# A 32-bit encoder block on one core: gate and up as seven half-token products of block sums, FFN in three groups

## What is computed

```
def rms_norm(x, g):
    xf = x.astype(jnp.float32)
    y = xf * lax.rsqrt(jnp.mean(xf * xf, axis=-1, keepdims=True) + NORM_EPS)
    return (y * g.astype(jnp.float32)).astype(x.dtype)

def swiglu(h, w_gate, w_up, w_down):
    return (jax.nn.silu(h @ w_gate) * (h @ w_up)) @ w_down
...
        x = x + 0.5 * swiglu(rms_norm(x, ffn1_norm[i]), ffn1_w_gate[i], ffn1_w_up[i], ffn1_w_down[i])
        h = rms_norm(x, mix_norm[i])
        proj = h @ w_in[i]
...
        x = x + jnp.concatenate([y_ssd, y_pool], axis=-1) @ w_out[i]
        x = x + 0.5 * swiglu(rms_norm(x, ffn2_norm[i]), ffn2_w_gate[i], ffn2_w_up[i], ffn2_w_down[i])
    return rms_norm(x, final_norm)
```

## Time and profile before

| | |
|---|---|
| median of 3 runs | 1042.38 us (1042.3 to 1042.4) |
| the profiled execution | 1042.32 us, of which the span from the first to the last instruction 1040.6 us |
| granted TensorE clock | 0.997 of full |
| busy: PE, DVE, ACT, POOL | 1031.2, 559.6, 380.4, 179.1 us |
| FFN1's first output tile is done, last unit of the mixer ends | VectorE reads their banks at 268.71 and 667.04 us |

### The profile page before, as it was taken

The page is one execution under the profiler, slowest core; times in us unless marked ns, Lnnn a source line. Parts: engine busy times, 40 slices in busy tenths (PEclk is TensorE's granted clock), DMA queues, the critical chain, the costliest instruction groups (busy, mean ns, idle before and its releaser), DMA issues.

```text
span 1040.6 us, 13577 instructions
## 1 busy us (share of the span) xinstructions
PE 1031.2 (99%) x4798; PEld 847.3 (81%) x4798; DVE 559.6 (54%) x686; ACT 380.4 (37%) x489; POOL 179.1 (17%) x166
## 2 busy tenths in 40 slices
PE   9999999999999999999999999999999999999997
PEld 7888888888888878878787888888888888888887
DVE  5544444444344468786799795554444444433432
ACT  6433223322333337652234753432333223332332
POOL 1110110101001032221063451110101101101100
PEclk9999999999999999999999999999999999999998
DMA  6533323322333343222222233333333332233222
GB/s 184 150 113 101 101 86 95 101 83 68 99 98 96 101 124 100 82 81 70 73 81 81 62 101 101 101 101 90 92 101 101 96 87 89 79 109 95 86 68 81
DMA packets 188873, 99.09 MB, mean 95 GB/s; under 512 B 3780, under 2 KB 188200, under 8 KB 188840
## 3 DMA queue, kind: packets, MB, share of 16 engines
q1 hardware_dynamic: 188168, 97.60, 32.3%
q10 hardware_dynamic: 672, 1.05, 0.3%
HBM read 96.54 MB, written 2.10 MB: 95 GB/s over the span
## 4 chain that ended last, share of the span: by engine, by line
PE 96%; DVE 3%; issue 1%; ACT 1%; POOL 0%; ACTq 0%; POOLq 0%
PE bank L1150 29%; PE bank L1152 29%; PE bank L1151 29%; PE bank L1222 1%; PE bank L1216 1%; PE bank L1219 1%; PE bank L1471 1%; PE bank L1284 0%; PE bank L1306 0%; PE bank L1472 0%; PE bank L1473 0%; PE bank L1274 0%; DVE w_lo_part L743 0%; DVE ebuf L903 0%; PE bank L1190 0%
## 5 line engine op out<-in xcount | busy, mean ns | idle before, releaser
L1150 PE MATMUL bank<-xghi,w_hi_part 128*128 128x512 f32 x960 | 377.4, 393 | 0.0
L1152 PE MATMUL bank<-xghi,w_lo_part 128*128 128x512 f32 x960 | 373.8, 389 | 0.0
L1151 PE MATMUL bank<-xglo,w_hi_part 128*128 128x512 f32 x960 | 373.6, 389 | 0.0
L743 DVE TENSOR_TENSOR w_lo_part<-w_raw,w_hi_part 128x1024 fp32r<-128x1024 f32 x194 | 253.9, 1309 | 192.8 <-ACT w_hi_part L498 187.5
L498 ACT ACTIVATE w_hi_part<-w_raw 128x1024 fp32r<-128x1024 f32 x194 | 203.8, 1051 | 196.2 <-PE bank L1152 194.7
L1150 PEld LDWEIGHTS bank<-xghi,w_hi_part 128*128 128x128 f32 x960 | 180.2, 188 | 39.9 <-issue 2.8
L1151 PEld LDWEIGHTS bank<-xglo,w_hi_part 128*128 128x128 f32 x960 | 180.3, 188 | 38.4 <-issue 1.2
L1152 PEld LDWEIGHTS bank<-xghi,w_lo_part 128*128 128x128 f32 x960 | 180.2, 188 | 37.5
L1150 PE MATMUL bank<-acthi,w_hi_part 128*128 128x512 f32 x330 | 130.5, 396 | 0.0
L410 POOL TENSOR_TENSOR gate_buf<-gate_buf,rstd 128x512 f32<-128x512 f32 x44 | 57.1, 1298 | 424.5 <-ACT gate_buf L521 424.5
L1152 PE MATMUL bank<-acthi,w_lo_part 128*128 128x512 f32 x330 | 129.4, 392 | 0.0
(11 more groups left out here) (223 smaller groups left out, 805.0 us busy)
## 6 DMA issues: line engine op xcount, KB each, us to landing
w_raw<-in_ffn_w_gate SPq DMA_DIRECT2D x42, 512.0 KB, 3.8
w_raw<-in_ffn_w_up SPq DMA_DIRECT2D x42, 512.0 KB, 3.8
w_raw<-in_w_in SPq DMA_DIRECT2D x29, 512.0 KB, 3.8
w_raw<-in_ffn_w_down SPq DMA_DIRECT2D x32, 384.0 KB, 3.2
w_raw<-in_ffn_w_down SPq DMA_DIRECT2D x32, 320.0 KB, 3.0
w_raw<-in_w_out SPq DMA_DIRECT2D x16, 512.0 KB, 3.6
out<-xtok SPq DMA_DIRECT2D x4, 512.0 KB, 3.4
xload<-in_x SPq DMA_DIRECT2D x3, 512.0 KB, 7.0
```

Of the source, the lines that this page charges most:

```text
L743: dve.tensor_tensor(wlo[:, slot(m)], raw[:, slot(m)], whi[:, slot(m)].bitcast(F32), ALU.subtract).then_inc(w_lo, 1)
L1150: pe.matmul(bank, w, h, start=first and n == 0, stop=False)
L1151: pe.matmul(bank, w, l, start=False, stop=False)
L1152: mm = pe.matmul(bank, wl, h, start=False, stop=last and n == blocks - 1)
```

## The change

**Gate and up.** For most hidden tiles two tiles are taken together (a quad: gate and up of two tiles, four raw weight slots). The 8 feature blocks are split into two halves of four, the two tiles are the other split, and the tokens are split into two halves of 256. The four weight quarters and the four activation quarters then make a 2 x 2 by 2 x 2 product, done with seven products instead of eight, on sums and differences of quarters. Each product is 24 matmuls of 256 columns: 8 for gate and up times four blocks, times 3 for the parts. Of the 22 tile pairs of both FFNs, 19 are quads; the first 4 tiles of FFN1 and the first 2 of FFN2 stay as they were ("direct").

**Sums of weights.** Four VectorE instructions of 128 x 1024 for a quad (`first_sum` to `fourth_sum`), and a high and a low part for each of the seven products. There are eight raw slots in place of four.

**Sums of activations.** Four combinations of 128 x 256 for each of four block pairs of `xT`, made once for an FFN: `halves_of_x` and `combination_hi` on ScalarE, `combine` and `combine_low` on VectorE. In FFN1 they stand in the four direct steps from the fifth item on; for FFN2 in the last four steps of the mixer.

**Results.** ScalarE copies three partial products out of PSUM, VectorE adds three later ones to them (`gather`), GpSimd scales three gates of 256 tokens by `rstd`.

**Groups.** Hidden tiles go in groups of 8, 8 and 6; behind each group all eight output tiles get that group's part. Each part is one unit of 8 or 6 blocks, scaled on VectorE by half of `rstd` into `upd` and added to `xT` in a second instruction. VectorE forms a weight's low part two items ahead of the running one, where it was three; ScalarE stays three ahead. In the last tile's halves only the third group's 6 blocks are left, where there were 22, and `finish` for the first half stands behind 3 blocks of the second half, where it stood behind 6. The loops of the FFNs are written out.

The core of the diff:

```diff
+        def weight(q, part):
+            quad = QUADS[q]
+            slot0 = quad.raw % RAW
+            if part in (SUM1, SUM4):
+                return wsum[:, 0]
+            if part == SUM2:
+                return wsum[:, 1]
+            f1, k1 = part in (SUM3, A22), part in (A12, A22)
+            pair = raw[:, slot0 + 2 * f1:slot0 + 2 * f1 + 2, :, :].rearrange("p e k f -> p e (k f)")
+            return pair[:, :, k1 * KH * P:(k1 + 1) * KH * P]
...
+                    sp.wait_ge(w_lo, FREE[key])
+                if key[0] == 1 and slot >= RING:
+                    sp.wait_ge(unit_done, M_FFN2)
...
+            def scale_gate(q, i, h, done, ready):
+                pool.wait_ge(done, q + 1)
+                gate = post[:, q % 2, i, 0:HALF]
...
+            def halves_of_x(f, j, gain):
+                act.wait_ge(x_ready, DK * 2 * f + j + 1)
+                act.activation(b12[:, j, :], xT[:, j * S + HALF:(j + 1) * S], ACT.Copy,
+                               scale=par[:, one(gain + j)]).then_inc(b12_ready, 1)
+            def combination_hi(f, j):
+                act.wait_ge(t_own, 4 * (KH * f + j + 1))
+                act.activation(thi[:, :, j, :], t32[:, j, :, :], ACT.Copy).then_inc(t_hi, 1)
...
+            def copy_product(q, part, i, bank, ready, reader):
+                act.wait_ge(unit_done, QUADS[q].base + part + 1)
+                if q >= 2:
+                    act.wait_ge(reader, q - 1)
+                act.wait_ge(t_lo, KH * (QUADS[q].ffn + 1))
+                act.activation(post[:, q % 2, i, :], PB[bank][:, :], ACT.Copy).then_inc(ready, 1)
...
+            def combine(f, j, gain):
+                c = 4 * (KH * f + j)
+                low, high = xT[:, cols(j)], xT[:, cols(j + KH)]
+                g0, g4, neg4 = par[:, one(gain + j)], par[:, one(gain + KH + j)], neg_gain[:, f, KH + j:KH + j + 1]
+                dve.wait_ge(b12_ready, KH * f + j + 1)
+                def term(i, x, scalar, other, op):
+                    dve.scalar_tensor_tensor(out=t32[:, j, i, :], in0=x, scalar=scalar, in1=other,
+                                             op0=ALU.mult, op1=op).then_inc(t_own, 1)
+                term(0, low[:, 0:HALF], g0, b12[:, j, :], ALU.subtract)
+                term(2, high[:, HALF:S], g4, b12[:, j, :], ALU.subtract)
+                dve.wait_ge(t_own, c + 1)
+                term(1, high[:, HALF:S], neg4, t32[:, j, 0, :], ALU.subtract)
+                dve.wait_ge(t_own, c + 3)
+                term(3, high[:, 0:HALF], neg4, t32[:, j, 1, :], ALU.subtract)
+            def combine_low(f, j):
+                dve.wait_ge(t_hi, KH * f + j + 1)
+                dve.tensor_tensor(tlo[:, :, j, :], t32[:, j, :, :], thi[:, :, j, :].bitcast(F32),
+                                  ALU.subtract).then_inc(t_lo, 1)
...
+            def first_sum(q):
+                for j in (2, 3):
+                    w_landed(dve, (QUADS[q].ffn, QUADS[q].raw + j))
+                if q:
+                    before = QUADS[q - 1].base + SUM4 + 1
+                    dve.wait_ge(w_lo, before)
+                dve.tensor_tensor(weight(q, SUM1), weight(q, SUM3), weight(q, A22), ALU.add).then_inc(sum_ready[1], 1)
...
+            def gather(q, part, i, bank, read, ready):
+                dve.wait_ge(unit_done, QUADS[q].base + part + 1)
+                dve.wait_ge(read, q + 1)
+                c = post[:, q % 2, i, :]
+                dve.tensor_tensor(c, c, PB[bank][:, :], ALU.add).then_inc(ready, 1)
...
+            def down_scaled(f, g, d, rows=slice(0, S), bank=None):
+                use = 3 * DK * f + DK * g + d
+                if use >= 2:
+                    added(use - 2)
+                dve.scalar_tensor_tensor(out=upd[:, d % 2, rows], in0=bank if bank is not None else PB[4 + d % 2][:, :],
+                                         scalar=0.5, in1=rstd[:, rows], op0=ALU.mult,
+                                         op1=ALU.mult).then_inc(d_read, 1)
...
+                        gate21(q)
+                    if product and it.part == SUM1:
+                        fourth_sum(q)
...
+                    if product and it.part == SUM3:
+                        gather(q, A12, 0, 3, p1_read, c11_done)
+                    if product and it.part == SUM4:
+                        gather(q, SUM3, 1, q % 2, p5_read, c22_done)
+                    if product and it.part == A22:
+                        gather(q, SUM4, 2, 2, u2_read, c12_done)
+                    if before is not None and before.kind == "direct":
+                        direct_post(f, before, n - 1)
+                    if before is not None and before.kind == "down":
+                        update(f, before.group, before.d, last)
+                    if starts_quad(n + 3):
+                        first_sum(ffn_item(n + 3).quad)
+                    if starts_quad(n + 2):
+                        second_sum(ffn_item(n + 2).quad)
+                    if converted <= n + 2 < M_FFN2 + len(FFN2):
+                        convert(n + 2)
+                    if before is not None and before.kind == "direct" and before.part:
+                        act_low(f, before.tile, before.tile % 2)
...
+                        combine_low(0, it.raw - RING)
+                    if chained and it.part == SUM1:
+                        act_even(q - 1)
+                    if chained and it.part == SUM2:
+                        act_low(f, QUADS[q - 1].tile, 0)
+                        act21(q - 1)
+                    if chained and it.part == A12:
+                        act22(q - 1)
+                    if chained and it.part == A22:
+                        act_low(f, QUADS[q - 1].tile + 1, 1)
+                    if starts_quad(n + 1):
+                        third_sum(ffn_item(n + 1).quad)
...
-                    dve.tensor_tensor(xT[:, cols(d)], PB[4 + j % 2][:, :], xT[:, cols(d)], ALU.add).then_inc(x_ready, 1)
-                    norm_lo(2, d, R_N2)
-                    convert(M + U_OUTS + j + RING, i)
+            for d in range(DK):
+                dve.wait_ge(unit_done, d + (M + U_OUTS + 1))
+                dve.tensor_tensor(xT[:, cols(d)], PB[4 + d % 2][:, :], xT[:, cols(d)], ALU.add).then_inc(x_ready, 1)
+                norm_lo(2, d, R_N2)
...
+            def last2(d):
+                if d >= 2:
+                    dve.wait_ge(sq_ready, d + (2 * DK - 1))
+                if d == 2:
+                    dve.wait_ge(gain_landed, 16)
+                    tokens(0, 0)
+                if d > 2:
+                    tokens(d - 2, d % 2)
...
+            def moving(f, part, k):
+                if part in (A11, A12, SUM4):
+                    t0 = (k + KH * (part != A11)) * S + HALF * (part == SUM4)
+                    return xghi[:, t0:t0 + HALF], xglo[:, t0:t0 + HALF]
+                i = {SUM1: 0, SUM2: 1, SUM3: 2, A22: 3}[part]
+                return thi[:, i, k, :], tlo[:, i, k, :]
...
+                pe.wait_ge(w_hi, n + 1)
+                pe.wait_ge(w_lo, n + 1)
+                for e in range(2):
+                    out = bank[:, half(e)]
+                    for k in range(KH):
+                        if part == SUM1 and local == 0 and e == 0:
+                            pe.wait_ge(t_lo, KH * f + k + 1)
+                        hi, lo = moving(f, part, k)
+                        w, wl = whi[:, slot(n), e * KH + k, :], wlo[:, slot(n), e * KH + k, :]
+                        end = k == KH - 1
+                        pe.matmul(out, w, hi, start=opens and e == 0 and k == 0, stop=False, skip_group_check=True)
+                        pe.matmul(out, w, lo, start=False, stop=False, skip_group_check=True)
+                        mm = pe.matmul(out, wl, hi, start=False, stop=end, skip_group_check=True)
+                mm.then_inc(unit_done, 1)
...
+                            down_part(f, it, n, early, True, False)
+                            down_part(f, items[r + 1], n + 1, early, True, False)
+                            down_part(f, it, n, late, False, True)
+                        elif it.d == 1:
...
+                            if it.d == 2:
+                                behind(0, 0)
+                            behind(it.d - 1, (it.d - 1) % 2)
+                            down_part(f, it, n, range(tiles // 2, tiles), False, True)
...
-                        first, last = j == 0 and k == 0, j == 3 and k == DOWN[3] - 1
-                        pe.matmul(bank, whi[:, slot(m), k, :], hi, start=first, stop=False)
-                        pe.matmul(bank, whi[:, slot(m), k, :], lo, start=False, stop=False)
-                        mm = pe.matmul(bank, wlo[:, slot(m), k, :], hi, start=False, stop=last)
-                    if j == 0:
+                for k in range(tiles):
+                    t0 = k * S + h * HALF
+                    hi, lo = acthi[:, t0:t0 + HALF], actlo[:, t0:t0 + HALF]
+                    bank = PB[LAST_BANK[h]][:, 0:HALF]```

```

(1 more changed line is left out.)

684 lines of the change are left out of this document (456 added, 228 removed).

## The result

| | before | after |
|---|---|---|
| median (4 runs each) | 1042.34 us (1042.2 to 1042.4) | 1050.77 us (1049.8 to 1052.44) |
| span of the profiled execution | 1040.6 us | 1049.8 us |
| granted TensorE clock | 0.997 | 0.986 |

The ratio is 1.0083, 95% interval 1.0065 to 1.01: the change makes the kernel 0.8% **slower**. The forecast of 1024 us had the wrong sign, and its range ended at 1041.

What follows compares the result with a forecast made beforehand. The prediction took PE, the matrix engine, as the bound: 1042.3 us, less 40.8 gained in 19 quads, plus 22.3 lost mostly at joints, gave 1023.8 us. Its forecast band was 1012 to 1033, its 8-in-10 range 1005 to 1041.

Steps and rivals of the forecast that it cites:

- Seven products: In the quads: 168 matmuls of 256 columns at 0.1155 us; 19.6 us a quad for 21.75, 40.8 us gained over 19.
- share of 0.46: In quads: cost to VectorE per microsecond of GpSimd overlap; with 1.95 us of GpSimd work, 0.9 us a quad.
- B: In quads: VectorE barely sets the pace, 20.4 us a quad, gain 25.7, 1039 us; chance 0.18.
- C: In quads: VectorE is the bound, every instruction costing its full duration, 21.6 us a quad, 1062 us; chance 0.08.
- Into FFN2: Mixer's last four steps: VectorE and ScalarE wait for each other, PE waits for `xglo`; 11.4 us lost (8 to 14).
- Into FFN1's quads: FFN1's items five to eight: the last combination comes after the second product wants it; 5.7 us lost (3 to 8).
- Into the mixer: Mixer's start: PE already waited 0.8 us for `xglo`, one more instruction is in front; 0.7 us lost.
- FFN2's group: FFN2's third group, `down`: transposes stand behind three blocks, 2.06 us, and wait for a 2.3 us chain; 1.7 us lost (0 to 3).
- tail: Kernel's end: two instructions in place of one, twice, and less matmul time over the first half's `finish`; 1.6 us lost (1 to 3).
- group ends: End of each of six groups: 0.2 us allowed each for the pair before the last activations; 1.2 us lost (0 to 3).
- D: In quads: written-out code keeps half-width matmuls from holding pace; at 0.125 us a quad is 21 us, 1050 us; chance 0.07.
- A: Joints are cheap, 13 us lost, and PE has the low pace, 19.1 us a quad; 1005 us; chance 0.17.

Runs made afterwards that it cites:

- all_x448: all_joints with the region of `acthi` and the combinations 448 bytes later, and `xghi` and `xglo` 448 bytes later too: 1018.26 us (0.9773).
- b_shift64: The kernel before, with only the region that holds `acthi` and `mixhi` moved 64 bytes later: 1047.47 us (1.0049).
- all_joints: The changed kernel with instructions reordered into FFN2, in both third groups and into FFN1's quads, none removed: 1024.36 us (0.9831).

## Why the prediction was wrong

The sum missed by 27.6 us of span. The largest part, 9.6, is FFN1's third group and the entry into the mixer, which the prediction put at 0.7; then 7.5 for the quads, 5.1 for unchanged work, which it put at nothing, and 3.2 and 1.9 for the entries into FFN1's quads and into FFN2.

**What bounds the kernel** was right: PE, in both kernels.

**Seven products, the term of the sum.** That half-width products pay, and that PE and not VectorE sets the pace, was right: PE has no gap in chained quads. The size was off: 20.0 us and not 19.6, 7.5 us over 19 quads. The step that failed is "I take the middle, 0.1155, since the trace gives no reason for the two paces". The upper row (0.1177) was nearer, and 0.119 lies above both. The trace of before did hold a hint: read tile by tile, 512 columns cost 0.2289 us on `acthi` and 0.2267 on `xghi`. So a distance is not the same for every tile, and the earlier trace rows, taken on `acthi`, was no price for new ones. That the two rows differ on one tile looks like the pair in all_x448, and what picks between them stays open.

**VectorE** was sized well, 18.4 forecast and 18.3 to 18.9 measured, but one input did not come out: a GpSimd instruction of 256, estimated at 0.65 us, is 1.65 long in the trace. In the rows above it starts beside VectorE's sum of weights, which keeps its normal 1.22 us, and it ends 0.6 us after that sum; the low part behind it takes 1.76 for 1.22. That is how two engines look that take turns, and it agrees with the rule of the Trainium skill (SBUF — State Buffer, "Who interferes with whom") better than the share of 0.46 that I took from the earlier trace rows. By these rows it costs VectorE 3 x 0.54 = 1.6 us a quad. Since PE was the bound, rivals B and C still fell; the quad near 20 us that the prediction derived from that rule came out for another reason, as PE had no gap.

**Unchanged work** was taken to keep its price. It didn't: 5.1 us, by the 64 bytes of `neg_gain`, which the diff shows and the prediction passed over. b_shift64 gives 5.3 for that alone.

**Into FFN2.** The mechanism was right to 2%: a step of 9.46 us where 9.65 was forecast, the last `xglo` 31.7 us after the first add (32.5). Lost were 13.3 and not 11.4; 1.8 of it is the clock that falls while PE waits, a term that the sum did not have at any joint.

**Into FFN1's quads.** 8.9 for 5.7. The waits, 1.9, 3.6 and 0.3 us, come to 5.8, about the 5.7 that was forecast; what the sum did not have is about 3 us of slow matmuls behind them (granted clock 0.50 from 67 to 71 us).

**Into the mixer** is the worst mis-reading: 0.7 forecast, 10.3 measured with the group ahead of it. I asked what the last step adds and not whether a step (4.91 us) is longer than its unit (4.2 us). Before, a tile had four units of which only the last carried these steps; now each unit of 18 matmuls does. Of the 7.0 lost at the entry 5.1 are PE's waits (0.3 before), and the granted clock is 0.50 from 380 to 386 us, so the matmuls behind the wait are slow, a cost that the sum lacked here too. (The 0.8 of the earlier trace rows is a wait of the weight load; the matmul itself waited 0.3.) For FFN2's group I had done this sum, and there it came out (1.4 for 1.7), as did the tail (2.1 for 1.6) and the group ends (1.3 for 1.2).

**Rivals.** D had nearly the right time (1050) with the wrong cause: the distance was 0.119, not 0.125, and in all_x448 three quads of the same written-out code ran their products on `xghi` at 0.1135, so the rate of instructions does not set 0.119. A's condition, cheap joints, is what all_joints made true, and it then gave 1024 and not 1005, since quads and 512-column units stayed dearer than A had them.

That all_joints lands on the forecast's 1024 confirms nothing: there dearer matmuls (7.5 and 5.1 us) and some 10 us of joint losses that are left stand where the forecast had 22.3 us of joint losses.

## What to carry over

When a bank's work is cut into smaller units, compare each unit's matmul time with the whole serial step that hangs on it; what is over adds up from unit to unit and comes out at the next stage. When two in-order engines hand results back and forth within a step, put other work between the halves before anything else: reordering alone was worth 26 us here. And read matmul distances tile by tile, since a new small tile shifts all that lie behind it; here one of 64 bytes was worth 5 us.

## What the runs showed of the hardware

- The distance between matmuls depends on the start address of the streamed tile; moves of the weights by 16 KB and more changed nothing. The same 512-column matmuls on `acthi` had 0.2289 us with the region at 110016 and 0.2333 at 110080; 448 bytes on, 0.2290 again. The best address for 512 columns was not the best for 256. The few layouts tried give no rule for choosing an address. At one address there can be two paces: `xghi` in all_x448 had about 0.1177 in most products and 0.1135 to 0.1139 in three quads, and `acthi` in the kernel before 0.1177 and 0.1133. What picks between them stays open.
- Behind each of the waits of 3.6, 4.5 and 8.5 us PE ran at a granted clock of 0.50 for another 3.7 to 4.9 us; filling the longest with small matmuls on an unused bank kept it at 1.00 and gave 1.8 us.
- A GpSimd instruction of 256 elements beside a busy VectorE took 1.65 us, longer than one of 512 in the earlier trace rows (1.30), which started while VectorE was idle.
